# Attention scores from rounded high and low parts on the whole array, in place of float32 products on half of it

## The reference

```
proj = h @ w_in                      # queries, keys, values, and the GLA inputs
aq, ak = rotary(aq), rotary(ak)      # 8 query heads, 2 key heads, 64 wide
s = einsum('bnqhgd,bnkhd->bnhgqk', qb, kw) * d ** -0.5
m = maximum(max(s), sink);  p = where(mask, exp(s - m), 0)
probs = p / (sum(p) + exp(sink - m));  o = probs @ v
```

## Time and profile before

| | |
|---|---|
| time, median of 3 runs | 2197.42 us (2196.26 to 2198.94) |
| span of the profiled execution | 2195.2 us (2.2 us under that median; its page gives no time around the span) |
| busy share: PE, DVE, ACT, POOL | 98%, 67%, 38%, 15% |
| chain of work that ended last | PE 94%, DVE 3%, DMA 1%, ACT 1%, issue 1% |
| score products (L2509), 64 rows x 384 columns | 96 records, 22.0 us busy in all |
| score products (L2509), 64 rows x 256 columns | 64 records, 11.2 us busy in all |

### The profile page before, as it was taken

How to read it: one execution, slowest core, us unless ns; L and a number is a source line. 1 busy time by engine, 2 the same in 40 slices (tenths; PEclk the granted TensorE clock), 3 DMA queues, 4 the chain that set the end, 5 groups by cost and what they waited for, 6 DMA issues and landing times.

```text
span 2195.2 us, 32680 instructions
## 1 busy us (share of the span) xinstructions
PE 2158.9 (98%) x11974; PEld 1913.5 (87%) x11974; DVE 1468.4 (67%) x2693; ACT 825.5 (38%) x1676; POOL 330.4 (15%) x325
## 2 busy tenths in 40 slices
PE   6999999999999999999999999999999999999998
PEld 5999999999888888877778888899999999988887
DVE  7666666666665686866653556777666666657576
ACT  7233222222343355655443324422222332333343
POOL 6111111111100002110002244212111111100000
PEclk8999999999999999999999999999999999999999
DMA  3322232233586565432245873132233223387554
GB/s 126 100 81 81 86 101 87 93 98 101 197 278 212 176 207 159 134 94 91 74 147 167 265 239 111 51 95 88 92 100 99 81 81 98 112 287 254 173 190 164
DMA packets 245746, 300.18 MB, mean 137 GB/s; under 512 B 24146, under 2 KB 159698, under 8 KB 245588
## 3 DMA queue, kind: packets, MB, share of 16 engines
q1 hardware_dynamic: 236948, 284.98, 40.8%
q10 hardware_dynamic: 8640, 13.11, 1.7%
HBM read 206.29 MB, written 88.47 MB: 134 GB/s over the span
## 4 chain that ended last, share of the span: by engine, by line
PE 94%; DVE 3%; DMA 1%; ACT 1%; issue 1%; SPq 0%; POOL 0%; POOLq 0%; DVEq 0%; ACTq 0%
PE ps L2331 16%; PE ps L2327 12%; PE ps L2329 9%; PE ps L2330 9%; PE ps L2341 8%; PE ps L2339 8%; PE ps L2340 8%; PE ps L2253 4%; PE ps L2255 4%; PE ps L2254 4%; PE ps L2271 1%; PE ps L2273 1%; PE ps L2272 1%; PE ps L2509 1%; PE ps L2520 1%; PE ps L2498 1%
## 5 line engine op out<-in xcount | busy, mean ns | idle before, releaser
L2331 PE MATMUL ps<-hs,w_lo 128*128 128x384 f32 (+1 forms) x992 | 305.6, 308 | 0.0
L2339 PE MATMUL ps<-w_hi,dh 128*128 128x512 f32 x770 | 300.3, 390 | 0.0
L2341 PE MATMUL ps<-w_hi,dh 128*128 128x512 f32 x770 | 299.8, 389 | 0.0
L2340 PE MATMUL ps<-w_lo,dh 128*128 128x512 f32 x610 | 237.4, 389 | 0.0
L1844 DVE TENSOR_TENSOR dh<-dr,dh 128x640 fp32r<-128x640 f32 x154 | 126.9, 824 | 160.4 <-ACT dh L1280 160.3
L1242 ACT CAST w_hi<-w_raw 128x512 fp32r<-128x512 f32 x220 | 135.8, 617 | 236.5 <-PE ps L2331 228.6
L2329 PE MATMUL ps<-hs,w_hi 128*128 128x384 f32 (+1 forms) x644 | 215.4, 334 | 6.1 <-DVE hs L1694 4.0
L2330 PE MATMUL ps<-hs,w_hi 128*128 128x384 f32 (+1 forms) x644 | 214.6, 333 | 0.0
L1280 ACT CAST dh<-dr 128x640 fp32r<-128x640 f32 x154 | 112.2, 728 | 268.1 <-PE ps L2341 250.8
L2327 PE MATMUL ps<-hs_first,w_hi 128*128 128x512 f32 x588 | 210.9, 392 | 0.3 <-DVE second_u L1786 0.2
L2327 PE MATMUL ps<-hs,w_hi 128*128 128x512 f32 x588 | 210.2, 391 | 0.0
(11 more groups left out here) (286 smaller groups left out, 4613.5 us busy)
## 6 DMA issues: line engine op xcount, KB each, us to landing
dr<-hid_mid SPq DMA_DIRECT2D x154, 320.0 KB, 3.2
w_raw<-in_w_ffn_down SPq DMA_DIRECT2D x176, 256.0 KB, 3.6
hid_mid<-st SPq DMA_DIRECT2D x88, 320.0 KB, 2.2
w_raw<-in_w_ffn_gate SPq DMA_DIRECT2D x44, 512.0 KB, 5.2
w_raw<-in_w_ffn_up SPq DMA_DIRECT2D x44, 512.0 KB, 5.1
hid_mid<-sg SPq DMA_DIRECT2D x66, 320.0 KB, 2.2
hq<-o_mid SPq DMA_DIRECT2D x70, 128.0 KB, 4.0
w_raw<-in_w_in SPq DMA_DIRECT2D x14, 512.0 KB, 4.9
```

The lines of the kernel that those rows point to most:

```text
L2331: last = mm(out, lo[:, k, :], b_hi, start=False, stop=k == 3, skip_group_check=True)
L2339: mm(out, hi, w_h, start=first and p in D_FRESH, stop=False, skip_group_check=True)
L2340: mm(out, hi, w_l, start=False, stop=False, skip_group_check=True)
L2341: return mm(out, lo, w_h, start=False, stop=last, skip_group_check=True)
```

## The change

The scores are computed from rounded parts too. For each head, one 128-partition operand holds the query's high part on the head's own 64 partitions and its low part on the other 64 (`Q_FIRST` for e=0, `Q_LAST` for e=1). The keys' high part stands on both halves of `K_HI[e]`, their low part on both halves of `K_LO[e]`; the second half is copied from the first by DMA (`keys_twice`). Two rounded products over the whole array, with `K_HI` and then `K_LO`, then give all four partial products of a head's scores.

- PE: a unit's two float32 products on 64 rows become four rounded ones on 128 rows. They wait for the low parts, and unit 0 for the doubled keys.
- ACT: ten casts of 64 x 1280, four of them (keys and pair 0) ahead of unit 0, the rest in pairs in units 4, 15 and 25 (`Q_SPLIT`). `gate_out(3)` moves from before unit 0 to behind `attend(0)`.
- DVE: ten subtractions of 64 x 1280, four ahead of `cumulate(3)`, the rest one each in units 5, 6, 16, 17, 26 and 27. The log gate is taken out of `cumulate` (`gate_logs`), which sets it ahead of the new work for head 3.
- SP: four transfers of 64 x 1280 for the doubled keys; loads for the first GLA head go to another buffer and in another order.

```diff
+            def keys_hi():
+                act.wait_ge(T["rot"], 3)
+                act.wait_ge(e_stored[0], 64)
+                for e in range(2):
+                    own = slice(e * HD, (e + 1) * HD)
+                    nc.scalar.copy(K_HI[e][own, :], kT[own, :]).then_inc(T["hi"], 1)
+            def queries_hi(j):
+                act.wait_ge(T["rot"], 3 * (j + 2))
+                for e, to in enumerate((q_first(j), q_last(j))):
+                    own = slice(e * HD, (e + 1) * HD)
+                    nc.scalar.copy(to[own, :], rotated(j + 1)[own, :]).then_inc(T["hi"], 1)
...
             split_in(7)
+            keys_hi()
+            queries_hi(0)
             move(5, 0)
             move(5, 1)
-            gate_out(3)
             move(5, 2)
             split_in(8)
...
+                if n == 0:
+                    gate_out(3)
+                if n in Q_SPLIT:
+                    queries_hi(Q_SPLIT.index(n) + 1)
...
+            def keys_lo():
+                for e in (1, 0):
+                    own = slice(e * HD, (e + 1) * HD)
+                    dve.wait_ge(T["hi"], e + 1)
+                    v.tensor_tensor(K_LO[e][own, :], kT[own, :], K_HI[e][own, :].bitcast(F32), ALU.subtract).then_inc(T["lo"], 1)
...
             for part in range(3):
                 rotate(1, part, q_rot[0], q_rot[0])
+            gate_logs(3)
+            keys_lo()
+            for e in range(2):
+                queries_lo(0, e)
             cumulate(3)
...
+            def keys_twice(of, done):
+                sp.wait_ge(T[done], 2)
+                for e in range(2):
+                    own, other = (slice(x * HD, (x + 1) * HD) for x in (e, 1 - e))
+                    sp.dma_start(of[e][other, :].bitcast(F32), of[e][own, :].bitcast(F32)).then_inc(T["twice"], 16)
...
-                    pe.wait_ge(T["rot"], j + 2)
+                    if n == 0:
+                        pe.wait_ge(T["twice"], 64)
+                    pe.wait_ge(T["lo"], 2 * (j + 2))
                     if n:
                         pe.wait_ge(T["p"], 2 * n)
-                    for e in range(2):
-                        half = slice(e * HD, (e + 1) * HD)
-                        last = mm(ps[:, e, 0:(hi - lo) * P], q_rot[j % 2][half, b * P:(b + 1) * P],
-                                  kT[half, lo * P:hi * P], start=True, stop=True)
+                    for e, q in enumerate((q_first(j), q_last(j))):
+                        scored, qb = ps[:, e, 0:(hi - lo) * P], q[:, b * P:(b + 1) * P]
+                        mm(scored, qb, K_HI[e][:, lo * P:hi * P], start=True, stop=False)
+                        last = mm(scored, qb, K_LO[e][:, lo * P:hi * P], start=False, stop=True)
                     last.then_inc(T["s"], 1)
```

More of the change, by code:

```diff
@@ L83 @@
 UNITS = PAIRS * TT
+Q_SPLIT = (4, 15, 25)
 GSTEPS = 42
@@ L273, in build @@
         go.append(place(4 * TOK * 4, "go_last", [P, TOK]))
+        K_HI = [place(4 * TOK * s, f"k_hi{e}", [P, TOK], F32R) for e, s in enumerate((4, 5))]
+        K_LO = [place(4 * TOK * s, f"k_lo{e}", [P, TOK], F32R) for e, s in enumerate((6, 2))]
+        Q_FIRST = [place(A_AT + 4 * TOK * s, f"q_first{j}", [P, TOK], F32R) for j, s in enumerate((3, 4))]
+        Q_LAST = [place(at, f"q_last{j}", [P, TOK], F32R) for j, at in enumerate((3 * 4 * TOK, 4 * TOK, A_AT + 2 * 4 * TOK))]
+        gla_tmp_first = place(8 * 4 * TOK, "gla_tmp_first", [P, TOK])
         with ExitStack() as s:
@@ L477, in build @@
         gn = named("gla_norm", "ld sum root normed turned scaled hi lo last_lo hi_stored lo_stored")
-        T = named("attn", "cs_ld sw_ld win_ld window products rot vT vN s negm p es norm turned "
+        T = named("attn", "cs_ld sw_ld win_ld rot hi lo twice vT vN s negm p es norm turned "
                           "pT_act pT_dve pv o_hi o_lo hi_stored lo_stored")
@@ L569, in build, with rotated, q_first, q_last @@
                   "gg0": ROW_GG, "gg1": ROW_GG + P, "gg2": ROW_GG + 2 * P, "gg3": ROW_GG + 3 * P}
+        def rotated(i):
+            return (kT, q_sw, q_sw, q_sw, q_raw)[i]
+        def q_first(j):
+            return Q_FIRST[j % 2]
+        def q_last(j):
+            return Q_LAST[(0, 1, 0, 2)[j]]
+        def keys_from(h):
+            return gla_tmp if h else gla_tmp_first
         first_chunks = (0, SEQ_CHUNKS[0])
@@ L1493, in _ @@
                         if IN_ORDER[w] == "aq2":
-                            act.wait_ge(T["products"], 2 * 3)
+                            act.wait_ge(T["rot"], 3 * 3 - 1)
                         if IN_ORDER[w] == "aq3":
-                            act.wait_ge(T["products"], 2 * 4)
+                            act.wait_ge(T["rot"], 3 * 4 - 1)
                         move(w, c)
@@ L1996, in rotate @@
             def rotate(i, part, to, src):
+                whole = rotated(i)
                 if part == 0:
@@ L2003, in rotate, with queries_lo @@
                         dve.wait_ge(T["s"], TT * (i - 2))
-                    v.tensor_tensor(to[:, :], src[:, :], cos[:, :], ALU.mult).then_inc(T["products"], 1)
+                    v.tensor_tensor(to[:, :], src[:, :], cos[:, :], ALU.mult).then_inc(T["rot"], 1)
                 elif part == 1:
-                    v.tensor_tensor(q_sw[:, :], q_sw[:, :], sin[:, :], ALU.mult).then_inc(T["products"], 1)
+                    v.tensor_tensor(q_sw[:, :], q_sw[:, :], sin[:, :], ALU.mult).then_inc(T["rot"], 1)
                 else:
[L2008 to L2012, removed]
+                    dve.wait_ge(T["rot"], 3 * i + 2)
+                    v.tensor_tensor(whole[:, :], to[:, :], q_sw[:, :], ALU.add).then_inc(T["rot"], 1)
+            def keys_lo():
[3 more added lines that the diff above has]
+                    v.tensor_tensor(K_LO[e][own, :], kT[own, :], K_HI[e][own, :].bitcast(F32), ALU.subtract).then_inc(T["lo"], 1)
+            def queries_lo(j, e):
+                of = (q_first(j), q_last(j))[e]
+                own, other = (slice(x * HD, (x + 1) * HD) for x in (e, 1 - e))
+                dve.wait_ge(T["hi"], 2 * (j + 1) + e + 1)
+                v.tensor_tensor(of[other, :], rotated(j + 1)[own, :], of[own, :].bitcast(F32), ALU.subtract).then_inc(T["lo"], 1)
+            for h in range(2):
+                gate_logs(h)
+                cumulate(h)
             for part in range(3):
                 rotate(0, part, kT, kT)
+            gate_logs(2)
             cumulate(2)
@@ L2082, in attend @@
                 if n in (22, 23, 24):
-                    rotate(4, n - 22, q_rot[1], q_raw)
+                    rotate(4, n - 22, q_raw, q_raw)
+                for j, at in enumerate(Q_SPLIT):
+                    if n - at in (1, 2):
+                        queries_lo(j + 1, n - at - 1)
             for n in range(UNITS - 8):
```

50 lines of the change are left out of this document (30 added, 20 removed).

## The result

The changed kernel takes 2203.57 us (median of 6 runs, 2202.9 to 2206.0), the kernel before 2196.84 us (6 runs, 2194.94 to 2199.32). The ratio is 1.0031, with a 95% interval of 1.0021 to 1.0041: slower by 6.7 us. The forecast was 2198.0, with a range up to 2203.0. The profiled execution of the changed kernel took 2206.0 us, with a span of 2204.2.

What follows compares the result with a forecast made beforehand. PE was taken to bound the kernel (94% of the chain of waits). Saving and stops summed as -6.2 + 4.2 + 1.2 + 1.2 + 0.2 = +0.6 us, giving 2198.0 us beside the median; range 2191.5 to 2203.

Steps and rivals of the forecast that it cites:

- PE's saving: PE in attention: 0.15 us less in each of 38 units with transposes, 0.5 for units 0 and 1, 6.2 us saved.
- First stop: DVE comes to unit 0 4.2 us late, at 941.9, so PE stops 4.2 us at unit 1's scores.
- The collision with POOL's correction: Ahead of unit 0, POOL's correction falls into head 3's scans on DVE and costs 1.5 us more.
- The doubled keys: Ahead of unit 0: transfers take 4.2 us and land by 934, ahead of 936.88, so PE doesn't wait.
- Second stop: At unit 2's scores: PE waits 1.2 us for unit 1's exponentials, which come behind `gate_out(3)` on ACT.
- ACT and DVE recover after unit 2: After the stop at unit 2, DVE (73% busy) and ACT (51%) recover in some units.
- Rival 3: PE's stop near unit 1 brings its clock down to 1.2 GHz: 2200.4 to 2203 us; chance 12%.
- The small stops: Up to unit 7: 1.2 us, estimated between 0 and 3; units 15, 16, 25 and 26: 0.2 us.
- Rival 4: ACT's casts in units 4, 15 and 25 lead to PE stops of 1.5 us at three places: 2202; chance 10%.

Runs made afterwards that it cites:

- Experiment 1: Kernel before with only its score products written as four rounded ones on data already there, no casts, subtractions, doubling or moves: 2191.59 us beside 2197.6, ratio 0.9972.
- experiment 7: Changed kernel with `gate_out(3)` alone put back in its old place, subtractions still ahead of head 3's scans: 2200.33 us, ratio 1.0010 to the kernel before.
- experiment 3: Changed kernel with 32 idle transposes on PE ahead of unit 1 and of unit 3: 2204.43 us, ratio 1.0032 to the kernel before.
- experiment 2: Changed kernel with pair 1's rotation in units 3 to 5 and unit 4's casts moved to unit 6: 2197.33 us, ratio 1.0002 to the kernel before.
- experiment 5: Kernel before with only `gate_out(3)` moved behind unit 0's exponentials: 2206.47 us, ratio 1.0042.
- experiment 6: Kernel before with `gate_out(3)` moved behind unit 0's exponentials and 32 idle transposes ahead of unit 3: 2203.2 us, ratio 1.0021.
- experiment 4: Changed kernel with the four early subtractions behind head 3's scans and `gate_out(3)` in its old place: 2198.33 us, ratio 1.0008 to the kernel before.
- experiment 8: Changed kernel with subtractions behind head 3's scans, `gate_out(3)` in its old place, pair 1's rotation in units 3 to 5: 2196.83 us, ratio 0.9997 to the kernel before.

## Why the prediction was wrong

**PE's saving, 6.2 us: right.** Experiment 1 gives 6.0, its trace 6.2, and both parts show in the late unit: transposes shorter by 0.17, scores longer by 0.02.

**First stop, 4.2 us: right, in part by luck.** DVE came to unit 0 at 942.21 (forecast 941.9), PE stopped 3.76 us. The collision with POOL's correction is there, but on another instruction: both scans take their 2.8 us, and the two little copies of L2041 behind them take 2.38 us instead of the 0.37 of experiment 7, so 2.0 us in place of 1.5. The sum came out even so (scans and centring 10.2 us, as forecast): the 3.38 us that I took for an undisturbed scan was itself beside a correction of POOL (921.87 to 924.38), and this 0.56 us is gone with the change.

**The doubled keys, no wait: slightly wrong.** The low parts' transfers were issued at 929.71 behind a weight load on SP and took 6.0 us to land, where I had counted 4.2: PE waits 0.52 us.

**Second stop, 1.2 us at unit 2, behind `gate_out(3)` on ACT: this step failed.** ACT's own order was as forecast: unit 1's exponentials end at 949.3 (949.1), and since PE was slowed by its clock it hardly waited there; with the clock held up (experiment 3) the wait is 0.84 us, so this part was about right. But what I named as queued behind `gate_out(3)` was ACT's work alone. The step left out the store of its result, and what waits for that store: a DVE operation in unit 1 with 1.8 us to spare. The store's lateness follows from rows of before and my own forecast: `gate_out(3)` done at 947.2 by the forecast, the issue 0.4 us on as before, 5.6 us to the landing, so 953.2 for a rotation that stands in DVE's queue at 947.0 (942.81 before, and 4.2 us later). So also the sentence failed that ACT and DVE recover after unit 2: the stop came at unit 3, with 4.3 us, and with the slow clock behind it u2 to u4 took 6.2 us more than in experiment 1. Experiments 2, 5 and 7 show this from three sides: take away the dependence, make it alone, undo it alone.

**Rival 3, the clock: the mechanism came, at both stops; the sum put it at nothing.** Behind the first stop u1 to u2 took 5.22 us, 1.4 more than in experiment 1; 0.5 of that goes away when the clock is held (4.75 in experiment 3), since then ACT's exponentials hold PE, and the second stop hid even this. Behind the second stop it was 1.5 us (u3 to u4 6.27, 4.78 in experiment 3), not hidden. The forecast of 2.4 and more took all 3.6 us of PE's work at half clock, but the clock was back at 0.91 in the window from 948 to 950. In experiment 5 the fall did cost 2.5 us (u3 to u4 7.40, 4.94 in experiment 6).

**The small stops, 1.2 and 0.2 us: right in size, by another cause.** Against experiment 1, units 6 to 8 take 1.0 us more and u26 to u27 0.4; units 15 to 25 lose nothing. I had named the two casts on ACT in unit 4. The trace shows a subtraction of unit 5 beside POOL's correction (972.51 to 974.90):

```profile
972.71 3.54 DVE L2076 TENSOR_TENSOR q_first<-q_sw,q_first 64x1280 fp32r<-64x1280 f32 x1
```

It takes 3.54 us in place of 1.49. The same holds in experiments 3, 4 and 7 (3.55 to 3.72 us), and all four kernels lose 1.0 to 1.1 us in units 6 to 8. In experiments 2 and 8, with that subtraction later, it takes 1.49 us and nothing is lost there. No experiment changes this alone, so the cause is likely, not shown. Rival 4's 1.5 us at each of three places did not come.

**The sum by the traces.** From unit 0's scores to unit 39's the form saves 6.2 us (experiment 1). The changed kernel takes 12.9 us more than experiment 1: 3.9 for u0 to u1 (first stop), 1.4 for u1 to u2 (clock), 4.7 for u2 to u3 (second stop), 1.5 for u3 to u4 (clock), 1.0 in units 6 to 8 and 0.4 at unit 26. That makes +6.7, and 6.7 us were measured. The 0.5 us for the doubled keys stands ahead of this stretch; it is inside the interval (about 2 us either way). The same account gives experiment 4 -2.3 us in the stretch (191.11) and 3.3 of stop ahead of it, +1.0 where 0.7 was measured. What the forecast's 6.8 us of stops lacked is the 6.2 us from unit 2 to unit 4: the late store, and the clock behind its stop.

## What to carry to other kernels

When an instruction moves, follow its result to the last reader, through stores and buffers that share addresses, and give each such wait its slack from the trace; a wait that shows as zero before may have 1.8 us to spare and be passed by 6. Look at what is queued behind the waiting instruction on its engine, since that is what stops the bounding engine. And work that doesn't fit ahead of the first unit need not go there: leaving the first pair in its old form gave up a quarter of the units and kept 5.0 of the 6.0 us.

## What the runs showed of the hardware

**Stops and clock.** In these kernels PE's clock went to 0.50 after stops of 3.76 (twice), 3.87, 4.27, 4.58 and 4.63 us and stayed at 1.00 after the one of 3.3. No length follows from this: near the start it kept 1.00 over one of 5.2 us, which ends at 18.87 in the window of the earlier trace rows.

**Transposes kept the clock up.** With 32 transposes of the identity in the place of the stop, PEclk stayed 1.00 in experiments 3 and 6, where it had been 0.50 without them. They are issued by the same call as the kernel's other transposes; the trace names both MATMUL and shows no mode. The Trainium skill (TensorE: Matmul & The Clock Gate, Part 4: PE-mode transpose) says that a transpose doesn't count as PE-busy in the same way; by that the clock should have fallen there as before. The measurement decides: here they counted.

**A tiny DVE operation can be held as long as a large one.** Beside POOL's correction of 128x1024 the two 64x10 copies of L2041 took 2.38 us, 0.37 in experiment 7; they ended at 940.08, 0.2 us after the correction (936.27 to 939.85). The kernel before had shown it already, beside a correction from 890.87 to 893.49:

```profile
891.34 2.38 DVE L1987 COPY to_mid<-gla_b 64x10 f32<-64x10 f32 x2
```

A 64x1280 scan lost as much there (4.85 us, in place of 2.82 undisturbed), and a 64x1280 subtraction above (3.54 in place of 1.49). The Trainium skill (SBUF — State Buffer, Who interferes with whom) describes DVE's and POOL's shared ports as a lock in which the second to issue is blocked until the first finishes; that fits a loss that doesn't depend on the size, and also that POOL's correction, which started while a scan ran, took 3.58 us in place of the 2.39 of the earlier trace rows.
